# A hybrid decoder layer on one core: last tile by halves, three rows added by GpSimd, first pieces from two queues, small products on four tiles, a spill copy moved

## The chip, the cores and the metric

The kernel runs on one core of a Trainium2 chip. The metric is the device time of one execution in microseconds (us), the median of three. The engines are TensorE (PE in the profile; its weight loads are PEld), VectorE (DVE), ScalarE (ACT), GpSimd (POOL) and SyncE (SP), which here only issues DMAs. They run their own instruction streams in order and meet at semaphores.

## The reference

One layer over 512 tokens of width 1024, all in float32:

```
h = rmsnorm(x);  proj = h @ w_in                    # in slots of 256 columns
A: RWKV-7 time mixing of the first columns (8 heads of 64, delta-rule state over the tokens)
B: gated short convolution
C: attention in 3 groups of 4 heads (window 128; dilations 4 and 16), ALiBi, merged by softmax of their sums
merged = sum_i sigmoid(gate_i) * (y_i @ w_branch[rows_i])
x = x + rmsnorm(merged @ w_out)
x = x + rmsnorm((silu(gate) * up) @ w_ffn_out)      # gate, up = rmsnorm(x) @ w_ffn_in
```

The last line is the tail of the kernel: for each row of 1024 outputs z, out = x + z * rsqrt(mean(z^2) + 1e-6) * norm_ffn_post.

## The kernel before, in words

**Slots.** All weights pass through two buffers of 1 MB (w_raw, even and odd slots). For each slot SP issues the load, ScalarE rounds it to w_hi (`high`, L688), GpSimd subtracts to w_lo in four quarters (`low`, L591), and TensorE multiplies three times with 128x128 weights: high by high, high by low, low by high (`three`, L1580 to L1582). Each such product streams 512 columns. SP loads slot n when w_lo of slot n - 2 is done.

**Start.** For slots 0 and 1 the operands come in six pieces (`PIECES`). On SP's queue stand, in this order, the parameters, and then for each piece a part of x_t, of w_in slot 0 and of w_in slot 1. ScalarE casts w_hi (L723), makes b_hi from x_t (L725) and casts slot 1 (L728). VectorE makes b_lo (L1039), GpSimd w_lo (L599). TensorE first runs ten products of ones (L1636), then waits for w_lo and b_lo of a piece before its three products.

**RWKV turns.** The tokens go in four turns T of 128. TensorE's stream in a turn is written by hand: small products of the recurrence, in f32, and between them products of the projection for later slots (`fill_steps`, L1695), so that TensorE has work while other engines prepare the next small operands. Small products with 64 contraction rows are put on tiles of the array. Each f32 product leaves two records in the profile. The keys' products (L1740) and loras (L1710) use a row half with all 128 columns: two heads, or two halves, are next to each other in the stream and use different row halves. Others (L1756, L1767, L1793) use four tiles of 64x64. The attention scores (L1881) are also on row halves.

**Spills.** The filled projection tiles leave PSUM through ScalarE: `evacuate(q)` copies bank 6 or 7 to spill_buf (L774); for odd q it also issues the DMA to `spill` (L777) and runs `next_high`, the cast of a coming slot (L688). TensorE may fill tile q when q - 1 copies of the turn are made (q counted from 0). At the end of a turn ScalarE squares y (L847), waits for the variance, takes the root (L849) and then, in turns 1 to 3, runs `evacuate(9)`, (10) and (11). VectorE makes y1 from the root with a reciprocal and five operations (L1347 to L1354). TensorE, when its fill products of the turn are issued, waits for y1 and transposes it (L1829).

**Tail.** The last slot's products are ordered by token tile t, 12 each, into two PSUM banks of 512 outputs. ScalarE squares the 1024 outputs of a tile with their sum (L692) and takes the root (L694). VectorE inverts it (L1026), scales the row by root and gain (L1027) and adds x1 (L1029). ScalarE then issues the store (L1012). The four tiles go through VectorE one after the other.

Of the kernel before, what the change touches and what calls it, by code (L numbers as in the profile page):

```python
# [25 lines left out]
def hybrid_layer(nc, x, norm_mix_post, norm_ffn_pre, norm_ffn_post, w_in, rwkv_w_up, rwkv_a_up, rwkv_g_up,  # L26
                 rwkv_ln_w, rwkv_ln_b, w_branch, w_out, w_ffn_in, w_ffn_out, x_t, channel_params, out, spill):
    F = mybir.dt.float32
# [71 lines left out]
    S_X, S_SIGMA, S_Z, S_EPS, S_SCRAP = 0, 8, 16, 60, 56  # L100

    with ExitStack() as ctx:
# [13 lines left out]
        w_lo = fixed("w_lo", [P, 2, SLOT], R)  # L116
        a_hi = fixed("a_hi", [P, KT, SEQ], R)
# [209 lines left out]
        row_ready = sem("row_ready")  # L327
# [96 lines left out]
        row_ones = chunk_run[:, 0:P]  # L424
        z_of = lambda t: ps[:, 2 * t:2 * t + 2].rearrange("p a b -> p (a b)")
# [32 lines left out]
        def _(sp):  # L458
# [19 lines left out]
            sp.dma_start(params[:, 0:N_PARAMS], channel_params).then_inc(params_loaded, 16)  # L478
            xt = x_t.rearrange("(k p) t -> p k t", p=P)
            for i, (k0, k1) in enumerate(PIECES):  # L480
                sp.dma_start(x_ct[:, k0:k1], xt[:, k0:k1]).then_inc(piece_loaded[i], 16)
                sp.dma_start(half8(0)[:, k0:k1], wi[0][:, k0:k1]).then_inc(piece_loaded[i], 16)
                sp.dma_start(half8(1)[:, k0:k1], wi[1][:, k0:k1]).then_inc(second_loaded[i], 16)
# [83 lines left out]
            sp.wait_ge(out_stored, 16 * NT)  # L567
# [14 lines left out]
        def _(pool):  # L582
# [87 lines left out]
            with pool.Fori(S_REST // 2 + 1, N_SLOTS // 2, 1) as i:  # L670
                for b in range(2):
                    low(i * 2 + b, b)

# [4 lines left out]
        def _(act):  # L678
# [37 lines left out]

            act.wait_ge(eps_ready, 1)
# [31 lines left out]
            def rwkv(T):  # L749
# [97 lines left out]
                s.activation(y2[:], y1[:], ACT.Square).then_inc(y_sq.sem, 1)  # L847
                need(y_var)
# [3 lines left out]
                if T > 0:  # L852
                    evacuate(9)
# [153 lines left out]
            for t in range(NT + 1):  # L1007
                if t < NT:
                    z_root_of(t, 1, N_SLOTS)
                if t > 0:  # L1010
                    act.wait_ge(row_ready, t)
                    act.dma_start(out[0].rearrange("(t p) d -> t p d", p=P)[t - 1], x1[:, t - 1]).then_inc(out_stored, 16)  # L1012
# [5 lines left out]
        def _(dve):  # L1018
# [4 lines left out]
            def add_normed(t, xin, gain, dst, done):  # L1023
# [3 lines left out]
                link(v.scalar_tensor_tensor(out=row[:], in0=z_of(t), scalar=stat[:, S_Z + t:S_Z + t + 1], in1=gain[:],  # L1027
                                            op0=ALU.mult, op1=ALU.mult))
                v.tensor_tensor(dst[:, t], xin[:, t], row[:], ALU.add).then_inc(done, 1)  # L1029
# [538 lines left out]
            for t in range(NT):  # L1568
                add_normed(t, x1, gain_ffn, x1, row_ready)
# [544 lines left out]
```

## Time and profile before

| | us |
|---|---|
| median of 3 runs | 968.93 (967.5 to 969.11) |
| the profiled execution | 967.39 |
| its span, first to last instruction | 965.7 |
| TensorE busy | 951.7 |
| VectorE, ScalarE, GpSimd busy | 529.2, 379.8, 432.6 |

The span is what the trace covers; the execution is 1.69 us longer. In the trace a line of the timeline gives the start, the duration, the engine, the source line, what is written from what, and in brackets how long the engine was idle before it and what ended the wait. Products on TensorE overlap their successors, so a product of 512 columns shows some 0.39 us while the next starts 0.23 us behind it. How long a piece of TensorE's stream takes is therefore read from start to start.

### The profile page before, as it was taken

The numbers are of one execution on the slowest core, as the hardware profiler recorded it, in microseconds if no ns is written. First come the engines' busy times: TensorE is split into PE (matmuls) and PEld (weight loads), VectorE is DVE, ScalarE is ACT, GpSimd is POOL, SyncE is SP. The second block draws the span as 40 slices with busy tenths as digits, with TensorE's granted clock in tenths as the row PEclk, the third lists the DMA queues.
The fourth block names the chain that finished last, engine by engine and source line by source line (L and its number), as shares of the span: only waits on it lengthen the run. The fifth ranks groups of instructions, "written<-read, shape, count | busy, mean of one in ns | idle before, by whom it ended". The sixth has DMA issues, their size and how long they took to land.

```text
span 965.7 us, 15061 instructions
## 1 busy us (share of the span) xinstructions
PE 951.7 (99%) x6138; PEld 770.9 (80%) x6138; DVE 529.2 (55%) x729; ACT 379.8 (39%) x518; POOL 432.6 (45%) x349
## 2 busy tenths in 40 slices
PE   9999999999999999999999999999999999999996
PEld 7887877887787788777778888888888888888885
DVE  5877876856577755889667639633333343300004
ACT  6424516533651562346653426523322233212112
POOL 4874424433272253343044754454455445544450
PEclk9999999999999999999999999999999999999999
DMA  8333322332333273237164652234333342233212
GB/s 279 115 99 119 104 94 88 131 132 69 128 133 111 87 252 135 74 126 267 68 218 152 240 189 73 77 98 114 102 87 87 97 117 90 88 104 114 88 44 87
DMA packets 107766, 117.74 MB, mean 122 GB/s; under 512 B 2880, under 2 KB 86848, under 8 KB 107712
## 3 DMA queue, kind: packets, MB, share of 16 engines
q1 hardware_dynamic: 99792, 100.70, 32.6%
q10 hardware_dynamic: 7920, 16.25, 4.4%
q8 instruction: 41, 0.67, 0.3%
q14 instruction: 13, 0.11, 0.0%
HBM read 100.70 MB, written 16.25 MB: 121 GB/s over the span
## 4 chain that ended last, share of the span: by engine, by line
issue 37%; PE 36%; POOL 22%; DVE 2%; ACT 1%; DMA 0%; POOLq 0%; SPq 0%; DVEq 0%; ACTq 0%
POOL w_lo L591 22%; PE ps L1580 12%; PE ps L1581 12%; PE ps L1582 12%; DVE x_ct L1135 1%; DVE row L1027 1%; DVE x L1029 1%; DVE rstd_x L1058 0%; DMA w_raw<-w_in 0%; DVE proj L1065 0%; ACT w_hi L688 0%; POOL wide_mask L638 0%; ACT L694 0%; ACT squares L692 0%; POOLq L652 0%
## 5 line engine op out<-in xcount | busy, mean ns | idle before, releaser
L591 POOL TENSOR_TENSOR w_lo<-w_raw,w_hi 128x512 fp32r<-128x512 f32 x296 | 411.5, 1420 | 495.0 <-ACT w_hi L688 494.6
L688 ACT CAST w_hi<-w_raw 128x2048 fp32r<-128x2048 f32 x74 | 141.1, 1906 | 146.2 <-PE ps L1582 123.3
L1695 PE MATMUL ps<-a_hi,w_hi 128*128 128x512 f32 x384 | 156.9, 409 | 1.0 <-ACT spill_buf L774 0.9
L1580 PE MATMUL ps<-a_hi,w_hi 128*128 128x512 f32 (+1 forms) x400 | 152.9, 382 | 0.2
L1582 PE MATMUL ps<-a_hi,w_lo 128*128 128x512 f32 (+1 forms) x400 | 152.2, 381 | 0.0
L1581 PE MATMUL ps<-a_lo,w_hi 128*128 128x512 f32 (+1 forms) x400 | 152.2, 381 | 0.0
L1695 PE MATMUL ps<-a_lo,w_hi 128*128 128x512 f32 x384 | 151.7, 395 | 0.0
L1695 PE MATMUL ps<-a_hi,w_lo 128*128 128x512 f32 x384 | 151.5, 394 | 0.0
L1580 PEld LDWEIGHTS ps<-a_hi,w_hi 128*128 128x128 f32 x400 | 75.2, 188 | 15.9 <-POOL w_lo L591 1.3
L1695 PEld LDWEIGHTS ps<-a_hi,w_hi 128*128 128x128 f32 x384 | 72.1, 188 | 19.2 <-issue 2.2
L1581 PEld LDWEIGHTS ps<-a_lo,w_hi 128*128 128x128 f32 x400 | 75.2, 188 | 14.3
L1582 PEld LDWEIGHTS ps<-a_hi,w_lo 128*128 128x128 f32 x400 | 75.2, 188 | 14.2
L1695 PEld LDWEIGHTS ps<-a_lo,w_hi 128*128 128x128 f32 x384 | 72.1, 188 | 16.3 <-issue 1.7
L1695 PEld LDWEIGHTS ps<-a_hi,w_lo 128*128 128x128 f32 x384 | 72.1, 188 | 15.8 <-ACT xs L831 0.7
L1550 DVE TENSOR_TENSOR f_gate<-ps,g_up 128x512 f32<-128x512 f32 x22 | 15.2, 691 | 115.5 <-PE ps L1582 115.2
L995 ACT ACTIVATE f_sig<-f_gate 128x512 f32<-128x512 f32 x22 | 13.9, 632 | 151.7 <-DVE f_gate L1550 151.7
L1581 PE MATMUL ps<-w_lo,f_hi 128*128 128x512 f32 x176 | 68.5, 389 | 0.0
L1580 PE MATMUL ps<-w_hi,f_hi 128*128 128x512 f32 x176 | 68.5, 389 | 0.0
L1582 PE MATMUL ps<-w_hi,f_lo 128*128 128x512 f32 x176 | 68.5, 389 | 0.0
L1026 DVE RECIPROCAL stat<-stat 128x1 f32<-128x1 f32 x4 | 0.6, 158 | 109.3 <-ACT stat L694 109.3
L774 ACT COPY spill_buf<-ps 128x512 f32<-128x512 f32 x36 | 21.0, 583 | 64.5 <-PE ps L1695 64.3
L1559 DVE TENSOR_TENSOR f_lo<-f_act,f_hi 128x512 f32 x22 | 27.1, 1230 | 23.7 <-ACT f_hi L1000 23.7
(319 smaller groups left out, 1524.8 us busy)
## 6 DMA issues: line engine op xcount, KB each, us to landing
w_raw<-w_in SPq DMA_DIRECT2D x32, 1024.0 KB, 5.1
w_raw<-w_ffn_in SPq DMA_DIRECT2D x44, 512.0 KB, 4.6
spill<-spill_buf ACTq DMA_DIRECT2D x27, 512.0 KB, 3.7
w_raw<-w_ffn_out SPq DMA_DIRECT2D x11, 1024.0 KB, 4.9
w_raw<-w_branch SPq DMA_DIRECT2D x5, 1024.0 KB, 8.2
g_ab<-spill SPq DMA_DIRECT2D x8, 512.0 KB, 4.7
w_raw<-w_out SPq DMA_DIRECT2D x4, 1024.0 KB, 7.4
proj<-spill SPq DMA_DIRECT2D x1, 3072.0 KB, 14.9
```

What stands on the lines that cost most here:

```text
L591: g.tensor_tensor(w_lo[:, b, c], w_raw[:, b, c], w_hi[:, b, c].bitcast(F), ALU.subtract).then_inc(lo_ready, 1)
L688: s.copy(w_hi[:, b], w_raw[:, b]).then_inc(hi_ready, 1)
L774: s.copy(spill_buf[:, b, half], ps[:, 6 + half]).then_inc(spill_copied, 1)
L995: s.activation(f_sig[:], f_gate[:], ACT.Sigmoid).then_inc(silu_sig, 1)
L1027: link(v.scalar_tensor_tensor(out=row[:], in0=z_of(t), scalar=stat[:, S_Z + t:S_Z + t + 1], in1=gain[:], op0=ALU.mult, op1=ALU.mult))
L1029: v.tensor_tensor(dst[:, t], xin[:, t], row[:], ALU.add).then_inc(done, 1)
L1550: v.tensor_tensor(f_gate[:], ps[:, bank], row_scale[:], ALU.mult).then_inc(f_gate_ready, 1)
L1559: v.tensor_tensor(lo_[:, i, b], f_act[:], hi_[:, i, b].bitcast(F), ALU.subtract).then_inc(f_lo_ready, 1)
L1580: t_.matmul(dst, w0, a0, start=first, stop=False)
L1581: t_.matmul(dst, w0, a1, start=False, stop=False)
L1582: return t_.matmul(dst, w1, a0, start=False, stop=last)
L1695: last = t_.matmul(ps[:, 6 + half], w[:, kt, half * P:(half + 1) * P], a, start=(kt == 0 and step == 0), stop=(kt == KT - 1 and step == 2))
```

## The change

Four edits in one diff.

1. **Tail.** For tiles 0 to 2 VectorE only inverts and scales the row (into two buffers in turn); GpSimd adds x1, and SP issues the store. The last tile's products are ordered by halves of 512 outputs. ScalarE squares the halves apart; the first half's mean goes into the bias of the root. VectorE multiplies each half by the gain, and at the end by the root with x1 added, in two halves; SP stores the two halves. ScalarE takes one scratch root ahead of the tail.
2. **Start.** The first piece of w_in (slots 0 and 1) and the parameters are issued from ScalarE's queue, the x_t pieces and the rest from SP's. TensorE runs the two high by high products of piece 0 when w_hi and b_hi are there, and the other four when the low parts are.
3. **Four tiles.** The keys' products, loras and scores write 64 output rows each, in place of 128, with twice as many products; four next to each other are on four 64x64 tiles.
4. **Spill copy.** In the last turn `evacuate(9)` stands between the squares of y and the root.

```diff
+                if i > 0:
+                    sp.dma_start(half8(0)[:, k0:k1], wi[0][:, k0:k1]).then_inc(piece_loaded[i], 16)
+                    sp.dma_start(half8(1)[:, k0:k1], wi[1][:, k0:k1]).then_inc(second_loaded[i], 16)
...
+            for t in range(NT - 1):
+                pool.wait_ge(row_scaled, t + 1)
+                g.tensor_tensor(x1[:, t], x1[:, t], norm_rows[t % 2][:], ALU.add).then_inc(row_ready, 1)
...
+            act.dma_start(first_part(0), first_rows[0][:, 0:1]).then_inc(piece_loaded[0], 16)
+            act.dma_start(params[:, 0:N_PARAMS], channel_params).then_inc(params_loaded, 16)
+            act.dma_start(first_part(1), first_rows[1][:, 0:1]).then_inc(second_loaded[0], 16)
             act.wait_ge(eps_ready, 1)
...
                 s.activation(y2[:], y1[:], ACT.Square).then_inc(y_sq.sem, 1)
+                if T == NT - 1:
+                    evacuate(9)
                 need(y_var)
                 s.activation(small[:, 48:48 + NH], small[:, 48:48 + NH], ACT.Sqrt).then_inc(y_std.sem, 1)
                 if T < NT - 1:
                     lora_inputs(T + 1)
-                if T > 0:
+                if 0 < T < NT - 1:
                     evacuate(9)
...
+            s.activation(stat[:, S_SCRAP:S_SCRAP + 1], stat[:, S_EPS:S_EPS + 1], ACT.Sqrt)
+            for t in range(NT - 1):
+                z_root_of(t, 1, N_SLOTS)
+            t = NT - 1
+            act.wait_ge(z_half_done, 1)
+            s.activation(squares[:, 0:SEQ], z_of(t)[:, 0:SEQ], ACT.Square, accum_out=stat[:, S_HALF:S_HALF + 1]).then_inc(half_squared, 1)
+            act.wait_ge(slot_used, N_SLOTS)
+            s.activation(squares[:, SEQ:D], z_of(t)[:, SEQ:D], ACT.Square, accum_out=stat[:, S_Z + t:S_Z + t + 1]).then_inc(z_squared, 1)
+            act.wait_ge(z_squared, 2 * NT)
+            act.wait_ge(half_bias, 1)
+            s.activation(stat[:, S_Z + t:S_Z + t + 1], stat[:, S_Z + t:S_Z + t + 1], ACT.Sqrt, bias=stat[:, S_HALF + 1:S_HALF + 2],
+                         scale=1.0 / D).then_inc(z_root, 1)
...
+            for t in range(NT - 1):
+                if t >= 2:
+                    dve.wait_ge(row_ready, t - 1)
+                root_inverted(t)
+                v.scalar_tensor_tensor(out=norm_rows[t % 2][:], in0=z_of(t), scalar=stat[:, S_Z + t:S_Z + t + 1], in1=gain_ffn[:],
+                                       op0=ALU.mult, op1=ALU.mult).then_inc(row_scaled, 1)
+            t, halves = NT - 1, (slice(0, SEQ), slice(SEQ, D))
+            dve.wait_ge(row_ready, t - 1)
+            dve.wait_ge(half_squared, 1)
+            v.tensor_scalar(stat[:, S_HALF + 1:S_HALF + 2], stat[:, S_HALF:S_HALF + 1], 1.0 / D, NORM_EPS,
+                            ALU.mult, ALU.add).then_inc(half_bias, 1)
+            v.tensor_tensor(norm_rows[t % 2][:, halves[0]], z_of(t)[:, halves[0]], gain_ffn[:, halves[0]], ALU.mult)
+            dve.wait_ge(z_squared, 2 * NT)
+            link(v.tensor_tensor(norm_rows[t % 2][:, halves[1]], z_of(t)[:, halves[1]], gain_ffn[:, halves[1]], ALU.mult))
+            root_inverted(t)
+            for c in halves:
+                row_out(t, c)
...
+            pe.wait_ge(piece_hi_ready, 1)
+            pe.wait_ge(b_hi_ready, 1)
+            first_high()
...
-                        for half in range(2):
-                            last = t_.matmul(ps[:, half, c], lora_up[own[half], c], xm[own[half], RT - 2], start=True, stop=True)
+                        for side in range(2):
+                            for half in range(2):
+                                last = t_.matmul(ps[own[side], half, c], lora_up[own[half], c][:, own[side]], xm[own[half], RT - 2],
+                                                 start=True, stop=True)
...
-                    for c in range(2):
+                    for c, side in ((0, 0), (0, 1), (1, 0), (1, 1)):
                         for h in (2 * j, 2 * j + 1):
-                            last = t_.matmul(ps[:, mt_bank(h), col:col + P], heads(bkd, h)[:, c * P:(c + 1) * P],
+                            last = t_.matmul(ps[own[side], mt_bank(h), col:col + P], heads(bkd, h)[:, kb:kb + HD],
                                              heads(ar, h)[:, c * P:(c + 1) * P], start=True, stop=True)
...
-                        for e in range(2):
+                        for side, e in ((0, 0), (0, 1), (1, 0), (1, 1)):
-                            last = t_.matmul(dst, q[:, n * P:(n + 1) * P], k[:, k0 * P:(n + 1) * P], start=True, stop=True)
+                            dst = ps[own[side], 2 * e + c0 // SEQ, c0 % SEQ:c0 % SEQ + width]
+                            last = t_.matmul(dst, q[:, q0:q0 + HD], k[:, k0 * P:(n + 1) * P], start=True, stop=True)
```

SP now issues the stores of rows 0 to 2 as each `row_ready` comes, and then the two halves of the last row as each `last_ready` comes.

## Rows read from the trace of the kernel before

**Rows 1.** The page, busy time, share of the span and records of TensorE.

```profile
PE 951.7 (99%) x6138; PEld 770.9 (80%) x6138; DVE 529.2 (55%) x729; ACT 379.8 (39%) x518; POOL 432.6 (45%) x349
```

**Rows 2.** Chain of waits, start: start us, us, what.

```profile
1.74 2.83 DMA w_raw<-w_in
```

**Rows 3.** Timeline, start to slot 2: start us, us, engine, line, operation.

```profile
4.95 0.61 PE L1636 MATMUL ps<-all_ones 128*128 128x128 f32 x3
...
6.69 0.47 PE L1580 MATMUL ps<-b_hi,w_hi 128*128 128x512 f32 x1 [1.13 <-DVE b_lo L1039]
...
27.11 5.03 POOL L591 TENSOR_TENSOR w_lo<-w_raw,w_hi 128x512 fp32r<-128x512 f32 x4 [3.22 <-ACT w_hi L688]
...
28.99 0.79 PE L1580 MATMUL ps<-b_hi,w_hi 128*128 128x512 f32 x1
```

**Rows 4.** Timeline of TensorE: groups of small products, each with its follower.

```profile
119.91 1.16 PE L1740 MATMUL ps<-ar,bkd 64*128 64x128 f32 x16
...
121.00 0.50 PE L1695 MATMUL ps<-a_hi,w_hi 128*128 128x512 f32 x1
...
228.33 0.69 PE L1793 MATMUL ps<-state,ar 64*64 64x64 f32 x32
...
228.96 0.50 PE L1695 MATMUL ps<-a_hi,w_hi 128*128 128x512 f32 x1
...
438.22 1.79 PE L1881 MATMUL ps<-proj 64*128 64x128 f32 x16
...
439.94 0.50 PE L1855 MATMUL ps<-a_hi,w_hi 128*128 128x512 f32 x1
```

**Rows 5.** Groups by line and shape, TensorE: count, busy us, mean ns.

```profile
L1740 PE MATMUL ps<-ar,bkd 64*128 64x128 f32 x128 | 9.3, 285 | 0.0
...
L1881 PE MATMUL ps<-proj 64*128 64x256 f32 x24 | 2.9, 376 | 0.0
```

**Rows 6.** Timeline, end of the last turn: ScalarE, VectorE, GpSimd, TensorE.

```profile
420.52 1.28 ACT L849 ACT_TABLE_LOAD   x1
...
421.82 0.21 ACT L849 ACTIVATE small<-small 128x8 f32<-128x8 f32 x1
...
422.55 0.50 PE L1695 MATMUL ps<-a_hi,w_hi 128*128 128x512 f32 x1 [0.91 <-ACT spill_buf L774]
...
422.75 0.20 DVE L1347 RECIPROCAL small<-small 128x8 f32<-128x8 f32 x1
...
422.99 1.91 ACT L688 CAST w_hi<-w_raw 128x2048 fp32r<-128x2048 f32 x1 [0.49 <-ACT spill_buf L774]
...
424.44 0.69 DVE L1351 TENSOR_TENSOR y<-y,ln_wb 128x512 f32<-128x512 f32 x1
...
424.98 4.68 POOL L591 TENSOR_TENSOR w_lo<-w_raw,w_hi 128x512 fp32r<-128x512 f32 x3 [12.16 <-ACT w_hi L688]
...
425.16 1.66 DVE L1352 TENSOR_TENSOR y<-y,y 128x512 f32<-128x512 f32 x1
...
428.58 0.66 PE L1829 MATMUL ps<-ident,y 128*128 128x128 f32 x4 [0.30 <-DVE y L1354]
```

**Rows 7.** Timeline, tail.

```profile
938.77 3.78 POOL L591 TENSOR_TENSOR w_lo<-w_raw,w_hi 128x512 fp32r<-128x512 f32 x3
...
949.09 1.03 ACT L692 ACTIVATE squares<-ps 128x1024 f32<-128x1024 f32 x1 [11.64 <-PE ps L1582]
...
950.22 1.28 ACT L694 ACT_TABLE_LOAD   x1
...
956.82 0.39 PE L1582 MATMUL ps<-w_hi,f_lo 128*128 128x512 f32 x1
...
957.41 1.28 DVE L1027 SCALAR_TENSOR_TENSOR row<-ps,stat,gain_ffn 128x1024 f32<-128x1024 f32 x1
...
961.38 1.22 DVE L1029 TENSOR_TENSOR x<-x,row 128x1024 f32<-128x1024 f32 x1
```

**Rows 8.** Stretches of the tail: us, busy by engine, granted clock, DMA share, GB/s.

```profile
961.00:962.00 1.00, 0.00 (x0) 0.00 (x0) 0.96 (x2) 0.00 (x0) 0.00 (x0) 0.50 1.00 410
```

More of the change, by code:

```diff
@@ L1567, in _ @@
             dve.wait_ge(gain_ffn_loaded, 16)
-            for t in range(NT):
-                add_normed(t, x1, gain_ffn, x1, row_ready)
+            for t in range(NT - 1):
+                if t >= 2:
[14 more added lines that the diff above has]
+                row_out(t, c)
         @block.tensor
@@ L1598, in by_channel, with by_token @@
                 return last
-            def by_token(n, b, ahi, alo, first, final, t, ks=(0, 1), ready=False):
+            def by_token(n, b, ahi, alo, first, final, t, ks=(0, 1), ready=False, halves=range(2)):
                 wh = w_hi[:, b].rearrange("p (k c) -> p k c", k=2)
@@ L1605, in by_token @@
                 for k in ks:
-                    for half in range(2):
+                    for half in halves:
                         if not ready:
@@ L1623, in turn_wide, with first_high, first_rest @@
                     last.then_inc(turned, 1)
+            def first_high():
+                for m in range(2):
+                    t_.matmul(ps[:, m], w_hi[:, 0, m * P:(m + 1) * P], b_hi[:, 0], start=True, stop=False)
+            def first_rest():
+                for m in range(2):
+                    c = slice(m * P, (m + 1) * P)
+                    t_.matmul(ps[:, m], w_hi[:, 0, c], b_lo[:, 0], start=False, stop=False)
+                    t_.matmul(ps[:, m], w_lo[:, 0, c], b_hi[:, 0], start=False, stop=False)
             def first_slots(n, ks, col_tiles):
@@ L1644, in _ @@
                     pe.wait_ge(b_lo_ready, k + 1)
-                    last = first_slots(0, (k,), range(2))
+                    if k == 0:
+                        first_rest()
+                    else:
+                        last = first_slots(0, (k,), range(2))
                 if i < TOGETHER:
@@ L2081, in _ @@
                         pe.wait_ge(f_read, N_FIN)
-                    last = by_token(S_FOUT + m, (S_FOUT + m) % 2, lambda k: f_hi[:, 2 * m + k], lambda k: f_lo[:, 2 * m + k],
-                                    m == 0, m == N_FOUT - 1, t, ready=i > 0)
+                    unit = lambda halves: by_token(S_FOUT + m, (S_FOUT + m) % 2, lambda k: f_hi[:, 2 * m + k], lambda k: f_lo[:, 2 * m + k],
+                                                   m == 0, m == N_FOUT - 1, t, ready=i > 0, halves=halves)
+                    if m == N_FOUT - 1 and t == NT - 1:
+                        unit((0,)).then_inc(z_half_done, 1)
+                        last = unit((1,))
+                    else:
+                        last = unit(range(2))
                     if m == N_FOUT - 1 and t < NT - 1:
```

43 lines of the change are left out of this document (22 added, 21 removed).

## The prediction, on record before the changed kernel was run

> **What bounds the kernel now.** Read first the page's busy shares: TensorE is busy for 951.7 of 965.7 us [rows 1], so the kernel is as long as TensorE's stream plus what stands ahead of it, behind it, and in its few stalls. The 14.0 us in which it is idle are read next from the timeline. Ahead: the first real product starts at 6.69, with 1.13 us of waiting for VectorE's b_lo, and the products that only warm the array end at 5.56 [rows 3]. Behind: the last product ends at 957.21 and the span at 965.7, 8.5 us later [rows 7]. In between there are few stalls; the two that matter here lie at 422.55 (0.91 us, for the spill copy of ScalarE) and at 428.58 (0.30 us, for y1) [rows 6]. So an edit pays in full where it shortens products or either end. It costs in full where it makes TensorE wait.
>
> **First pieces.** Before, piece 0 of x_t is issued second and that of w_in third on SP: issued at 1.74, landed 2.83 later, at 4.57 [rows 2]. Now SP begins with x_t and ScalarE's queue with the w_in piece, both at about 0.8, so that the piece lands near 3.6. ScalarE has three issues first (some 0.46 each) and then its table load and scratch activation (1.28 + 0.2), which ends near 3.7: no loss. Operands are thus 0.93 earlier: b_lo lets TensorE go at 5.76, not 6.69. The two high products need only b_hi; TensorE reaches them when the warm ones are out of its way (5.4 to 5.56) and streams them in 2 x 0.213 (512 columns at 2.4 GHz), to about 5.85. What is left starts 0.84 earlier and is 0.43 shorter: 1.27. Does it keep that? At slot 2 TensorE starts at 28.99, and GpSimd's first quarter is ready at 27.11 + 5.03/4 = 28.37 [rows 3]: 0.62 of slack. That quarter follows the transfers, which move up by 0.46 (one issue less ahead of the stream) to 0.93. So between 1.08 and 1.55 us survive. I take 1.15 us gained; bounds 0.6 (the two products still run at the pace of the warm ones, which took about twice what 2.4 GHz allows, and slot 2 waits) and 1.4. The later pieces go through SP with three issues less ahead, and no queue is longer.
>
> **Four tiles.** The count of products in keys' products, loras and scores doubles, each half as wide in its weights. A group of 16 records of 128 columns on two row halves takes 1.09 us from its first start to the next 128x128 product; a scores group of 16 records, 12 of them of 256 columns, takes 1.72 [rows 4]. The 0.63 between them is six times 128 more columns in each row half: 0.105 per 128 columns, so both halves already stream beside each other. Fixed part: 1.09 - 8 x 0.105 = 0.25. A group that runs on four 64x64 tiles, 32 records of 64 columns, takes 0.63 [rows 4]: 8 per tile at 0.053 is 0.42, fixed part 0.21. So the new group is 8 x 0.105 + 0.21 = 1.05, a gain of 0.04. Groups: 128/16 = 8 of keys' products, 4 of loras (16 records in each turn), 4 of scores [rows 5]: 16 x 0.04 = 0.6. No group lies next to another of the same tile shape, before or after, so there are as many changes of shape as before. Bound above: if all of the 0.63 grew with the columns, a new group would be 1.26 and cost 0.17; in units of 128 columns the groups are 8 + 4 + 2 x 1.75 + 2 x 2 = 19.5, so 3.3 us lost. Bound below: 1 us gained. I take 0.55 gained, for the four-tile row is the nearest of kind.
>
> The trace thus shows four tiles streaming at once at 64 columns. The Trainium skill (TensorE: Matmul & The Clock Gate, Part 3, what overlaps and what doesn't) says that a weight load overlaps running matmuls only where its row group differs. By that rule the two column tiles of a row half would take turns; the four-tile row, 0.63 where turns would need at least 0.85, speaks against it. It is a rival below, priced from rows.
>
> **The spill copy moved.** In the last turn evacuate(9) now stands ahead of the square root that y1 needs. It is three things, not one: the copy (128x512 from PSUM, 0.58 as the mean of its group on the page), its DMA issue, for which ScalarE stood idle 0.49, and the next_high behind it, a cast of 1.91 [rows 6]. What they need is there by 420.5: the bank's products ended with the half slot before, some 5 us earlier, and the cast's weights had landed. The copy is done near 421.1, so TensorE's stall of 0.91 (1.05 in its pace) goes and its last fill product ends near 427.1. But the root, with its own table load of 1.28, which started at 420.52 and 421.82, now follows the cast: cast from 421.6, table load at 423.4, root at 424.7, 2.9 later. VectorE had other work until 422.75 (0.7 of slack behind the root), so its reciprocal moves from 422.75 to 425.0: 2.25 later. Behind it five such operations lead to y1. Two that lay beside GpSimd's w_lo took 1.66, one that did not 0.69 [rows 6]. GpSimd's quarter set is now 1.4 earlier against TensorE while the chain is 2.25 later; about two and a half products lie beside it instead of two, 0.3 more. TensorE's turn of y1 stood at 428.58 and waits for exactly this chain, now until about 431.1. What is late next is thus y1, and the stall that went was in front of that wait and bought nothing. Cost 2.5 us; bounds 0 (the chain has slack that I don't see) and 2.9. TensorE idles some 3.9 us there. All that follows in the attention part hangs on y_a or on TensorE and moves along.
>
> **The tail.** Before, VectorE did reciprocal, scaled row (1.28) and add (1.22) of four rows back to back and ended at 962.60; the table load of 1.28 at 950.22 was on that path [rows 7]. Now the table is loaded earlier, in ScalarE's idle time. Row 0's root comes at 950.5, rows 1 and 2 when their tiles are done; scaled rows end near 952.1, 954.8, 957.6. GpSimd adds: its w_lo quarter of 512 columns takes 3.78/3 = 1.26 [rows 7], so 1024 take some 2.5, beside VectorE's scaled rows, which read PSUM. Adds end near 954.7, 957.4, 960.2. Last tile: the first half is squared before the last product ends; the second half near 958.0 (half of 1.03, and the read of the sum); root at 958.35. VectorE: bias at 957.7, two half products (about 0.68 each) to 959.2, reciprocal to 959.4, then two half rows: one beside GpSimd's last add, some 1.1, one alone, 0.7: 961.1, 1.5 before the old end. The stores are now SP's, in order: row 2 at 960.3, halves at 960.8 and 961.2. They are 1 MB together; at 410 GB/s [rows 8] 2.6 us from 961.2, so done near 963.8, where the old last store of 0.5 MB needed 3.1 us in all from 962.6 to 965.7. With the same rest of about 0.9 behind the data: 964.7. Gain 1.0 to 1.3; I take 1.1. Bounds: 2.0 (the stores don't queue behind each other) and 0.7 lost (each add 3.7, as in the rival).
>
> **Sum.** -1.15 - 0.55 + 2.5 - 1.1 = -0.3 us. It is made against the profiled execution, 967.39 (span 965.7 and 1.69 around it), which gives 967.1. The median of the runs, 968.93, is 1.54 above that execution; the difference carried over gives 968.6. The change gains at both ends about what it loses in the middle.
>
> **Rivals.**
> *The root is not late (chance 0.17).* Were y1's chain not longer (the table load and root ahead of the cast, or slack on VectorE), the middle would cost nothing: -2.8, 966.1. For it: TensorE has hardly a wait there now. Against it: 0.30 us of wait for y1 even before the change, ScalarE in program order, and a chain on VectorE with 0.7 of slack.
> *TensorE's clock falls in the new gap (0.15; the case on the slower side).* The granted clock is at its half level (1.2 of 2.4 GHz) in the stretch 961 to 962, after a last product that ended at 957.21 [rows 7, 8], so it had fallen within 3.8 us without products. The new gap at 427 is 3.9 us by my sum. At the start the warm products, from 1.16 to 5.56, still went at half pace at the end, and the products at 6.69 did not [rows 3]: over 4.2 us of work at half pace, 2.1 to 2.8 us lost, so +2.1 in all: 971.0. It decides from a gap about as long as the one in the tail. Against it: the gap is 0.1 longer than the bound that I can read, no more.
> *GpSimd's adds bound the tail (0.07).* If an add beside VectorE takes 3.7 (as 1.66 to 0.69 for VectorE's own), three end at 963.2 and the span 3.1 later: 0.7 lost instead of 1.1 gained, 970.4. Against it: the scaled row reads PSUM.
> *Column tiles of a row half take turns (0.03).* Each group's stream doubles: 19.5 x 0.84 = 16.4 us lost, 985.
> *The likeliest (0.55)* has its own range of 967.2 to 970.2; 0.03 is left for what I don't see.
>
> **Chances.** A difference under 0.2% (1.94 us) can't be told from none here. Faster, below 967.0: the first rival and a little of the likeliest (a tail or four tiles at their good ends), 0.25. Slower, above 970.9: two thirds of the clock case, the column tiles, and some of the likeliest and of the adds, 0.19. Same: 0.56. Range for 8 in 10: 965.7 to 971.2.
>
> **What would show it.** First product at about 5.5 and the stream whole to slot 2; groups of keys' products at 1.05, not 1.09 (0.85 more means turns); at the last turn the ScalarE order copy, cast, table load, root, no wait at the last fill, and a wait for y1 of 3 to 4 us, with the clock in it; GpSimd's adds at 2.5 each, last half row near 3.9 us behind the last product, end of the span about 7.4 behind it. The prediction is wrong if the wait for y1 is under 1 us, or if the clock falls.

## The result, and the profile after: 0.2% slower, with the clock fallen in the new gap

| | before | after |
|---|---|---|
| median, 20 runs each on one chip | 967.48 (967.0 to 969.35) | 969.64 (969.23 to 971.9) |
| ratio of after to before, 95% interval | | 1.0021 [1.0015, 1.0027] |
| the profiled execution's span | 965.7 | 967.5 |
| last product starts | 956.82 | 959.93 |
| from its end to the end of the span | 8.5 | 7.2 |

The predicted 968.6 was built on a median of 968.93, which is high: 20 runs of the kernel before give 967.48. Thirteen of these 20 took 967.0 to 967.9 and seven 968.3 to 969.4, for a reason that nothing here shows, and two of the three runs behind the prediction were of the longer kind. The fair comparison is of differences: forecast -0.3 us, measured +1.8 between the two profiled executions and +2.2 between the medians. The range held the time, but by luck: moved to the base of 967.48 it would have ended 0.1 above the result. The direction did not hold.

The page's line of TensorE, which answers to [rows 1]: 288 more records, and 0.9 us more of busy time although the span is 1.8 longer.

```profile
PE 952.6 (98%) x6426; PEld 770.4 (80%) x6426; DVE 521.3 (54%) x729; ACT 380.0 (39%) x521; POOL 440.1 (45%) x352
```

The start. First the head of the chain of waits (start, us, what), in the place of [rows 2]; then the timeline, in the place of [rows 3].

```profile
1.27 3.63 DMA params<-channel_params
```

```profile
4.92 0.40 ACT L742 CAST w_hi<-w_raw 128x256 fp32r<-128x256 f32 x1 [1.19 <-DMA params<-channel_params]
...
6.10 1.12 PE L1672 MATMUL ps<-b_hi,w_hi 128*128 128x512 f32 x2 [0.30 <-ACT b_hi L744]
...
7.06 0.40 PE L1678 MATMUL ps<-b_lo,w_hi 128*128 128x512 f32 x1
...
28.89 0.79 PE L1624 MATMUL ps<-b_hi,w_hi 128*128 128x512 f32 x1
```

The chain no longer begins with a piece of weights but with the parameters. Issued second on ScalarE's queue, they landed at 4.90; x_t's piece had landed at 3.7 and the w_in piece at 4.1, both ahead of the 4.57 of before. The two high products do start 0.59 earlier than the first product did, but stand 0.56 and 0.40 us ahead of what follows them, the pace of the warm ones or worse. The low products wait for b_lo, which is ready at 6.82 (6.54 before), and so start at 7.06. Slot 2 starts at 28.89, 0.10 earlier than before. That is within what equal starts differ by from kernel to kernel (below).

The small groups, in the place of [rows 4]:

```profile
115.76 1.10 PE L1804 MATMUL ps<-ar,bkd 64*64 64x128 f32 x32
...
116.80 0.50 PE L1757 MATMUL ps<-a_hi,w_hi 128*128 128x512 f32 x1
...
441.79 1.74 PE L1945 MATMUL ps<-proj 64*64 64x128 f32 x32
...
443.47 0.50 PE L1919 MATMUL ps<-a_hi,w_hi 128*128 128x512 f32 x1
```

The keys' products' group by shape (duration min/median/max in ns, first and last start), in the place of [rows 5], has 256 records, twice as many:

```profile
L1804 PE MATMUL ps<-ar,bkd x256: 268/269/321, 115.8 to 375.0; 64*64 64x128 f32 x128
```

A group of keys' products takes 1.04 from start to follower (1.09 before), a group of scores 1.68 (1.72).

The end of the last turn, in the place of [rows 6]:

```profile
419.23 0.63 ACT L866 ACTIVATE y<-y 128x512 f32<-128x512 f32 x1 [9.60 <-DVE y L1364]
...
419.77 0.57 ACT L793 COPY spill_buf<-ps 128x512 f32<-128x512 f32 x1
...
420.83 1.91 ACT L702 CAST w_hi<-w_raw 128x2048 fp32r<-128x2048 f32 x1 [0.49 <-ACT spill_buf L793]
...
422.76 1.28 ACT L870 ACT_TABLE_LOAD   x1
422.82 5.89 POOL L602 TENSOR_TENSOR w_lo<-w_raw,w_hi 128x512 fp32r<-128x512 f32 x4 [10.64 <-ACT w_hi L702]
...
424.05 0.21 ACT L870 ACTIVATE small<-small 128x8 f32<-128x8 f32 x1
...
424.36 0.20 DVE L1376 RECIPROCAL small<-small 128x8 f32<-128x8 f32 x1 [2.29 <-ACT small L870]
...
424.60 1.31 DVE L1377 TENSOR_TENSOR y<-y,small 128x512 f32<-128x512 f32 x1
...
425.94 1.65 DVE L1379 TENSOR_TENSOR y<-y,ln_wb 128x512 f32<-128x512 f32 x1
...
430.76 1.12 PE L1893 MATMUL ps<-ident,y 128*128 128x128 f32 x4 [4.36 <-DVE y L1383]
```

ScalarE's order is copy, cast, table load, root. The wait for the spill copy is gone and one of 4.36 us for y stands behind it. The turn of y starts at 430.76; it had been 428.58. Then the same stretch of the stream is slower too. Stretches of 2 us: length, busy of PE, PEld, DVE, ACT, POOL, then granted clock, DMA share, GB/s:

```profile
430.00:432.00 2.00, 1.24 (x5) 1.24 (x6) 1.47 (x5) 0.09 (x1) 0.23 (x1) 0.56 0.18 12
432.00:434.00 2.00, 2.00 (x7) 1.54 (x7) 1.90 (x8) 2.00 (x4) 1.17 (x3) 0.58 0.82 298
434.00:436.00 2.00, 2.00 (x10) 1.65 (x9) 1.06 (x4) 2.00 (x5) 1.63 (x4) 1.00 1.02 362
```

The granted clock is at its half level (1.2 GHz) for most of 430 to 434, behind 4.36 us without products. It fell some 3.9 us behind the end of the last product (426.41), still within the wait. From the turn of y to the first scores the stream takes 441.79 - 430.76 = 11.03; before, it took 438.22 - 428.58 = 9.64. The clock costs 1.39.

The tail, in the place of [rows 7]:

```profile
957.95 2.40 POOL L686 TENSOR_TENSOR x<-x,row_next 128x1024 f32<-128x1024 f32 x1 [0.25 <-DVE row_next L1601]
...
959.93 0.39 PE L1626 MATMUL ps<-w_hi,f_lo 128*128 128x512 f32 x1
...
962.15 2.15 DVE L1057 SCALAR_TENSOR_TENSOR x<-row_next,stat,x 128x512 f32<-128x512 f32 x2
...
963.66 1.09 SPq L577 DMA_DIRECT2D out<-x  x2
```

```profile
964.00:965.00 1.00, 0.00 (x0) 0.00 (x0) 0.30 (x1) 0.00 (x0) 0.00 (x0) 0.50 1.01 406
```

GpSimd's adds take 2.4 each. The second fence is the stretch of the last stores, in the place of [rows 8]: 406 GB/s. The last half row ends 4.0 behind the last product's end, and the span 7.2 behind it, against 8.5. The clock falls in every tail too, but not at one distance from the last product. Two of the kernels below show it, the one with four tiles and tail alone and then the one with the late w_lo on one queue; their last products ended at 956.73 and 957.15:

```profile
958.00:959.00 1.00, 0.00 (x0) 0.00 (x0) 0.93 (x3) 0.00 (x0) 1.00 (x1) 0.91 0.90 365
```

```profile
962.00:963.00 1.00, 0.00 (x0) 0.00 (x0) 0.00 (x0) 0.00 (x0) 0.00 (x0) 0.65 0.96 361
```

A mean of 0.91 puts the fall at 958.8, 2.1 behind the last product; a mean of 0.65 puts it at 962.3, 5.2 behind. In the tails of the 14 traces kept, the fall came 2.1 to 5.2 us behind the last product.

**The account.** Up to the squares of y the kernel is 0.64 earlier (419.87 to 419.23): 0.1 from the start, the other 0.54 from the small groups (12 of them at some 0.05). From the squares to the turn of y it is 2.82 longer, the clock costs 1.39, and from the first scores to the last product it is 0.46 shorter. So the last product is 3.11 later. The tail gives 1.31 back: +1.80.

### The profile page after: what moved, and what is told of

Its sections match the earlier page's. It is cut to its first block, busy times and chain, and to the rows that moved or that the text cites. A ratio compares the mean times of both kernels' runs of the same rounds, so it can differ in the third digit from the quotient of the medians.

```text
span 967.5 us, 15649 instructions
## 1 busy us (share of the span) xinstructions
PE 952.6 (98%) x6426; PEld 770.4 (80%) x6426; DVE 521.3 (54%) x729; ACT 380.0 (39%) x521; POOL 440.1 (45%) x352
## 4 chain that ended last, share of the span: by engine, by line
PE 75%; issue 13%; POOL 7%; DVE 3%; ACT 1%; DMA 0%; ACTq 0%; POOLq 0%; DVEq 0%
PE ps L1757 26%; PE ps L1624 14%; PE ps L1626 14%; PE ps L1625 14%; POOL w_lo L602 7%; PE ps L1831 1%; PE ps L1804 1%; DVE proj L1198 1%; PE ps L1794 1%; PE ps L1857 0%; PE ps L1872 0%; PE ps L1773 0%; PE ps L1780 0%; PE ps L1825 0%; DMA params<-channel_params 0%
```

## The experiments

Each was timed in five rounds beside the kernel before on one chip. Times are medians; ratios are to the kernel before, with the 95% interval.

### The spill copy back in its place

```diff
-                if T == NT - 1:
-                    evacuate(9)
                 need(y_var)
...
-                if 0 < T < NT - 1:
+                if T > 0:
                     evacuate(9)
```

> The changed kernel with evacuate(9) of the last turn behind the root again. Theory: the move made y1 2.8 us late against TensorE's stream and the wait of 4.4 us let TensorE's clock fall, for 1.4 us more. So here no wait for y1 over 0.5 us, granted clock 1.00 throughout, span 963.2 to 963.6 (967.5 before the edit), time 2 us below the kernel before. Rival: start, four tiles or tail cost the time; then the span stays at 967 or more.

Measured: 965.70, ratio 0.9978 [0.9969, 0.9987], span 964.1.

```profile
428.25 0.66 PE L1891 MATMUL ps<-ident,y 128*128 128x128 f32 x4 [0.30 <-DVE y L1381]
...
437.41 1.07 PE L1927 MATMUL ps<-ident,proj 128*128 128x128 f32 x8 [0.32 <-DMA proj<-spill]
```

The clock stays at 1.00 up to the tail, and the wait for y is 0.30. The other three parts together are worth 0.22%; with the moved copy they are a loss of 0.21%. The moved copy costs 3.4 us of span, more than its own delay of 2.8. The span was forecast as 963.2 to 963.6, so 0.5 is missing. A new wait shows as well: the stream now arrives before the loads from `spill` have landed, which SP issues when y is ready.

### The moved copy alone, on the kernel before

```diff
+                if T == NT - 1:
+                    evacuate(9)
                 need(y_var)
...
-                if T > 0:
+                if 0 < T < NT - 1:
                     evacuate(9)
```

> The kernel before with only evacuate(9) of the last turn moved ahead of the root. Theory: y's turn 2.8 us later, a wait of 4.4 us, the granted clock at half for some us behind it: span 965.7 + 2.8 + 1.2 = 969.7, time 4 us above the kernel before. Rival: it costs this only together with the earlier start or the four tiles; then 2 us or less.

Measured: 972.37 (5 runs), ratio 1.0056 [1.0042, 1.0069], span 970.2. The turn of y, and one stretch of 2 us:

```profile
431.69 0.96 PE L1831 MATMUL ps<-ident,y 128*128 128x128 f32 x4 [4.34 <-DVE y L1356]
```

```profile
432.00:434.00 2.00, 2.00 (x8) 1.71 (x7) 1.75 (x8) 1.31 (x4) 0.47 (x2) 0.50 0.63 161
```

The same wait and the same half level, without any other part of the change; the forecast span was 969.7, and slot 2 began 0.62 later here than in the kernel before (29.61, held by GpSimd's w_lo). The clock fell at 431.9, 0.2 behind the start of the turn. The stretch from the turn of y to the scores takes 11.29, 1.65 more than before.

### The gap filled with products

```diff
                 need(y_ready)
...
+                    need(y_mid)
+                    for _ in range(16):
+                        t_.matmul(ps[:, 0], a_hi[:, 0, 0:P], a_hi[:, 0], start=True, stop=True)
```

The changed kernel with 16 products in the wait for y, whose results nothing uses.

> The changed kernel with 16 further products of 512 columns (3.6 us, their result is not used) in TensorE's wait for y1 in the last turn. Theory: the wait ends at the same place, near 430.8, but the clock stays at 1.00 and the 1.4 us behind it are saved: span 966.1, time 968.2. Rival: the stretch behind the wait is slow because the other engines are late, not for the clock: span 967.5 as in the changed kernel.

Measured: 968.09, ratio 1.0003 [0.9994, 1.0012], span 966.4.

```profile
430.00:432.00 2.00, 1.24 (x9) 0.88 (x7) 1.49 (x5) 0.27 (x1) 0.23 (x1) 1.00 0.00 0
432.00:434.00 2.00, 2.00 (x10) 1.68 (x9) 1.86 (x6) 2.00 (x4) 1.29 (x4) 1.00 0.80 257
```

The clock stays at full, and from the turn of y to the scores it takes 9.66 (431.04 to 440.70), as before the change. The turn itself starts 0.28 later than in the changed kernel. So the slow stretch was the clock's and not that of late engines, the rival's reason. The clock is a cost of its own, 1.1 us of span net, and it turns no measurable difference into a slower kernel.

### The copy alone ahead of the root, cast behind it

```diff
                 if T == NT - 1:
-                    evacuate(9)
+                    evacuate(9, (0,))
                 need(y_var)
...
-                if 0 < T < NT - 1:
-                    evacuate(9)
+                if T > 0:
+                    evacuate(9, (0, 1) if T < NT - 1 else (1,))
```

Part 0 is the copy; part 1 is its DMA issue and the cast.

> The changed kernel with only the copy of evacuate(9) ahead of the root; its DMA issue and the cast stand behind the root. Theory: the cast (1.91) and the issue (0.5) are what makes y1 late; the copy alone (0.57) fits in the 0.7 that the root has. So the root is 0.6 later than at first, y1 at most 0.2, TensorE's wait of 0.9 for the copy goes and turns up as a wait of 1.0 to 1.4 for y1: span within 0.3 of the one with the move undone, near 963.4. Rival: the copy itself sets y1: span 965 or more.

Measured: 967.75, ratio 1.0000 [0.9991, 1.0009], span 964.7. Its runs spread from 966.08 to 969.16, and the profiled one (966.43) is among the shortest.

```profile
421.68 0.21 ACT L875 ACTIVATE small<-small 128x8 f32<-128x8 f32 x1
...
423.77 6.33 POOL L602 TENSOR_TENSOR w_lo<-w_raw,w_hi 128x512 fp32r<-128x512 f32 x4 [11.56 <-ACT w_hi L702]
423.83 1.77 DVE L1385 TENSOR_TENSOR y<-y,ln_wb 128x512 f32<-128x512 f32 x1
425.64 1.66 DVE L1386 TENSOR_TENSOR y<-y,y 128x512 f32<-128x512 f32 x1
...
429.02 0.66 PE L1898 MATMUL ps<-ident,y 128*128 128x128 f32 x4 [2.58 <-DVE y L1388]
```

The root is in time again and y is still late. The cast now follows the root at once (421.80, against 422.99 in [rows 6]), so GpSimd starts its w_lo 1.2 earlier too, and three of VectorE's five operations on y lie beside it instead of two. The copy was cheap; what followed it in each order was not. The span was forecast near 963.4.

In the profiled run the clock stood at 1.00 behind the wait of 2.58. The mean granted clock of the other runs says that this was not the rule: it is 0.998 in three runs (966.1 to 966.4, the profiled one among them) and 0.996 in the other eight (967.7 to 969.2). The changed kernel, where the clock fell, has 0.994 to 0.996 in all of its 20 runs, and the kernel with the copy back 0.997 to 0.999. So the clock very likely fell in this gap as well, in eight runs of eleven; no trace of one of the eight was kept.

### The whole spill step ahead of the squares

```diff
-                if T == 0:
+                if T in (0, NT - 1):
...
-                if T == NT - 1:
-                    evacuate(9)
                 need(y_var)
```

Here `evacuate(9)` stands where turn 0 has its own, before the squares, while ScalarE is idle.

> The changed kernel with evacuate(9) of the last turn ahead of the squares of y, where ScalarE stood idle for 9.6 us. Theory: copy, issue and cast fit in the idle time; no wait for the copy, y1 not late, and GpSimd's w_lo is done before the products on VectorE that lead to y1, which then take 0.69 instead of 1.66: y's turn 1 to 2 us earlier than with the move undone, span 961.5 to 962.5. Rival: the cast's weights land too late and ScalarE squares late: span no better than 963.4.

Measured: 965.61, ratio 0.9980 [0.9971, 0.9989], span 963.7.

```profile
418.81 6.01 POOL L602 TENSOR_TENSOR w_lo<-w_raw,w_hi 128x512 fp32r<-128x512 f32 x4 [6.45 <-ACT w_hi L702]
...
421.29 2.38 DVE L1371 TENSOR_TENSOR y<-uv,small 64x512 f32<-64x512 f32 x2
...
428.33 0.66 PE L1891 MATMUL ps<-ident,y 128*128 128x128 f32 x4 [1.75 <-DVE y L1381]
```

GpSimd's w_lo moves with the cast and now slows other operations of VectorE in the same chain (2.38 here, 1.38 in the changed kernel). The turn of y stays where it was with the copy back (428.33 and 428.25). The forecast span of 961.5 to 962.5 missed, and not by the rival: ScalarE squared y on time.

### That w_lo held until y is ready

```diff
-            with pool.Fori(3, S_REST // 2 + 1, 1) as i:
+            with pool.Fori(3, S_REST // 2, 1) as i:
                 for b in range(2):
                     low(i * 2 + b, b)
+            low(S_REST - 1, 0)

             pool.wait_ge(y_ready.sem, NT)
+            low(S_REST, 1)
             g.iota(step_i[:], [[-1, P]], base=0, channel_multiplier=1).then_inc(dist_ready, 1)
```

> The changed kernel with two edits at the end of the last turn: ScalarE runs evacuate(9) ahead of the squares of y instead of between squares and root, and GpSimd makes w_lo of slot 31 only after y1 is ready (before, it starts as soon as the cast is done, and then lies beside VectorE's five operations on y). My theory (what delays y is the cast ahead of the root, and what lengthens it is GpSimd beside VectorE, 0.69 to 1.66 us each): with both gone the five operations take 0.69 each, y is ready near 426, TensorE has no wait above 0.3 us at the end of the turn, its clock stays at 1.00, the spill loads are issued some 2 us earlier, and the time is 3 to 4.5 below that of the kernel before: 963 to 964.4 (span 962.0 to 963.2). Rival: TensorE is held elsewhere; w_lo of slot 31 comes 4 to 5 us later and TensorE's products of that slot wait for it, so nothing is gained over the copy alone ahead of the squares: 965.6 (span 963.7).

Measured: 966.13, ratio 0.9984 [0.9975, 0.9993], span 964.4.

```profile
426.16 5.03 POOL L602 TENSOR_TENSOR w_lo<-w_raw,w_hi 128x512 fp32r<-128x512 f32 x4 [13.84 <-DVE y L1383]
...
431.47 0.24 DVE L1146 CAST step_f<-step_i 128x128 f32<-128x128 int32 x1 [5.40 <-POOL step_i L670]
...
443.34 1.74 PE L1945 MATMUL ps<-proj 64*64 64x128 f32 x32 [1.80 <-DVE p_buf L1418]
```

My account of y was right: all five operations took 0.69, y was ready at 426.1, its turn came at 426.41, and the scores 1.2 earlier than in the version above. My time was wrong, and not for the rival's reason (TensorE's wait for w_lo was 0.6). GpSimd's iota, the seed of the attention's distance tables, stood behind the held w_lo, so VectorE's tables were late, and TensorE waited 1.80 for p_buf. The gain had become a wait 17 us further on.

### The iota ahead of that w_lo

```diff
             pool.wait_ge(y_ready.sem, NT)
-            low(S_REST, 1)
             g.iota(step_i[:], [[-1, P]], base=0, channel_multiplier=1).then_inc(dist_ready, 1)
+            low(S_REST, 1)
```

> The kernel with the late w_lo of slot 31, and GpSimd's iota (0.25 us), from which VectorE builds the distance tables of the attention, stands ahead of that w_lo instead of behind it. In the kernel with the late w_lo the turn of y came at 426.4 and the first scores at 436.8, 1.2 earlier than with the copy alone moved, but VectorE got the iota at 431.1 instead of 428.4, its tables ended at 439.9 and TensorE waited 1.80 us for p_buf. My theory (that wait is the tables' chain): it goes, the tables are done before 436.5, the last scores of the group start near 462.9 instead of 464.6, and the span is 962.8 to 963.3, some 1.2 to 1.6 below that of the late w_lo; a wait of 0.3 to 0.8 us for the spill loads or w_lo may be left. Rival: the tables are slow because they lie beside GpSimd's w_lo (0.43 for 0.23), whichever comes first, and p_buf stays late by over 1 us: span 964 or more.

Measured: 965.45, ratio 0.9981 [0.9972, 0.9990], span 963.5.

```profile
426.14 5.03 POOL L602 TENSOR_TENSOR w_lo<-w_raw,w_hi 128x512 fp32r<-128x512 f32 x4
426.28 1.22 DVE L1146 CAST step_f<-step_i 128x128 f32<-128x128 int32 x1 [0.41 <-POOL step_i L669]
427.53 1.22 DVE L1147 TENSOR_SCALAR rem_i<-step_i 128x128 int32<-128x128 int32 x1
...
428.78 1.22 DVE L1148 TENSOR_SCALAR ahead_f<-step_f 128x128 f32<-128x128 f32 x1
...
436.53 1.07 PE L1929 MATMUL ps<-ident,proj 128*128 128x128 f32 x8 [0.55 <-DMA proj<-spill]
```

The wait for p_buf fell to 0.22. The span is 0.9 below the version above, where I had said 1.2 to 1.6, and at 963.5 just outside my 962.8 to 963.3; the waits for w_lo (0.8) and the spill loads (0.55) are what is left. The rival named a real effect (VectorE's small operations take 1.22 beside GpSimd) of no consequence, as there was time.

### Four tiles and tail, with start and spill copy as before

```diff
-            act.dma_start(first_part(0), first_rows[0][:, 0:1]).then_inc(piece_loaded[0], 16)
-            act.dma_start(params[:, 0:N_PARAMS], channel_params).then_inc(params_loaded, 16)
-            act.dma_start(first_part(1), first_rows[1][:, 0:1]).then_inc(second_loaded[0], 16)
...
-            first_high()
...
-                    if k == 0:
-                        first_rest()
-                    else:
-                        last = first_slots(0, (k,), range(2))
+                    last = first_slots(0, (k,), range(2))
```

with SP's queue and `evacuate(9)` as in the kernel before.

> The changed kernel with the start's and the spill's edits undone: four tiles and tail alone. Theory: four tiles gain 0.03 to 0.04 us in each of 16 groups, 0.6 in all, the tail 1.3: span 963.8 to 964.0, so 0.5 below the tail alone, and the same within 0.2 as the kernel with only the spill move undone (964.1), since the start gave nothing. Rival: the start gave its 1.1 us and something else took it: then this kernel is a microsecond slower than that one.

Measured: 965.59, ratio 0.9984 [0.9975, 0.9993], span 963.9.

```profile
4.40 0.41 ACT L737 CAST w_hi<-w_raw 128x256 fp32r<-128x256 f32 x1 [2.09 <-DMA w_raw<-w_in]
...
28.80 0.79 PE L1617 MATMUL ps<-b_hi,w_hi 128*128 128x512 f32 x1
```

On one queue the first cast starts 0.5 earlier than on two, and slot 2 no later. Forecast and span agree (963.8 to 964.0), and with the start's part the same kernel had 964.1 (medians 965.59 and 965.70). The start's part is worth nothing that these two can tell apart.

### The tail alone

The kernel before with the tail of the changed one (GpSimd's adds, last tile by halves).

> The kernel before with the tail's edit alone. Theory: from the last product's end to the end of the span 7.2 us instead of 8.5, nothing else moves: span 964.4, time 1.3 us below the kernel before. Rival: the stores at SP's end or GpSimd's adds eat half of it: 0.6 or less.

Measured: 966.07, ratio 0.9988 [0.9979, 0.9997], span 964.5: 1.2 below the kernel before, as forecast. Its last product ends at 957.32 and its span 7.2 behind that. This and the kernel above leave 0.6 of span for the four tiles; that kernel also had a wait of 0.47 for the spill loads, which this one has not. But the two starts differ as well: here slot 2 began at 29.46, held by GpSimd's w_lo, and there at 28.80. So the 0.6 is not the four tiles' alone.

### The parameters first on SP's queue, spill copy back

```diff
+            sp.dma_start(params[:, 0:N_PARAMS], channel_params).then_inc(params_loaded, 16)
...
-            act.dma_start(params[:, 0:N_PARAMS], channel_params).then_inc(params_loaded, 16)
```

> The changed kernel with the spill move undone, and with the parameters issued first on SP again (x_t's piece 0 second there, the w_in pieces still on ScalarE's queue). Theory: the start gained only 0.1 us because the parameters, issued second on ScalarE's queue beside the big pieces, landed 3.65 us after their issue instead of 1.7, at 4.91, and held up ScalarE. Here they land near 2.5, x_t's piece near 4.1, ScalarE casts at 4.1 instead of 4.9, and slot 2 starts at 28.2 to 28.5 instead of 28.9 to 29.1: span 0.5 to 0.9 below the kernel with only the spill move undone (964.1). Rival: later pieces or GpSimd's w_lo for slot 2 limit it: slot 2 stays at 28.9 or later and the span at 964.

Measured: 965.54, ratio 0.9978 [0.9969, 0.9987], span 964.6.

```profile
4.89 0.41 ACT L742 CAST w_hi<-w_raw 128x256 fp32r<-128x256 f32 x1 [1.64 <-DMA x_ct<-x_t]
...
6.06 0.70 PE L1670 MATMUL ps<-b_hi,w_hi 128*128 128x512 f32 x2 [0.86 <-ACT b_hi L744]
...
437.93 1.06 PE L1927 MATMUL ps<-ident,proj 128*128 128x128 f32 x8 [1.20 <-DMA proj<-spill]
```

The parameters now landed at 3.0 and the w_in piece at 3.2, and x_t's piece, now issued second, took the parameters' place: it landed at 4.81, and the cast starts at 4.89, against 4.92. Slot 2 started at 28.81 and y's turn 0.37 earlier than with the parameters on ScalarE's queue (427.88 to 428.25), but TensorE waited 1.20 for the spill loads in place of 0.32. This profiled run (966.37) is the longest of eleven, so its span is no measure; the medians, 965.54 and 965.70, do not show the 0.5 to 0.9 that I had forecast. The number is the rival's, the reason is not: GpSimd's first quarter for slot 2 began at 26.57 and was done a microsecond before TensorE came to it.

### One queue, high products first, on the two later versions

```diff
-                if i > 0:
-                    sp.dma_start(half8(0)[:, k0:k1], wi[0][:, k0:k1]).then_inc(piece_loaded[i], 16)
+                sp.dma_start(half8(0)[:, k0:k1], wi[0][:, k0:k1]).then_inc(piece_loaded[i], 16)
...
-            act.dma_start(first_part(0), first_rows[0][:, 0:1]).then_inc(piece_loaded[0], 16)
```

> As the kernel with the late w_lo, but the first pieces are all on SP's queue in the order of the kernel before; only the two high products first are kept of the start. My theory (the first pieces land no earlier from two queues, since the transfers behind them share the same transfer engines; 4.57 on one queue, about 4.9 on two): the real products start a little earlier than on two queues, slot 2 starts at 28.4 to 28.6 instead of 28.8, and the span is 0.2 to 0.5 below that kernel's. Rival: slot 2 is held by GpSimd's quarter and the loads behind the first pieces, so it starts at 28.8 to 29.1 on either arrangement and the spans agree within 0.2.

> As the kernel with the iota ahead of the late w_lo, but all first pieces on SP's queue in the order of the kernel before, with the two high products first. My theory (two queues land the first pieces no earlier): slot 2 starts 0.1 earlier than on two queues, as it did with the late w_lo alone (28.94 to 29.05), and the spans agree within 0.3. Rival (that queue matters and the difference was hidden by the later wait for p_buf): the span is 0.5 or more from that of the same kernel on two queues.

Measured, with the late w_lo: 965.76, ratio 0.9981 [0.9972, 0.9990], span 964.3 (964.4 on two queues), slot 2 at 28.94 (29.05). With the iota ahead of it: 965.22, ratio 0.9974 [0.9965, 0.9983], span 963.4 (963.5), slot 2 at 28.66 (28.81). The first of these had been forecast to gain 0.2 to 0.5 of span and start slot 2 at 28.4 to 28.6; that missed, on the rival's side in the numbers. Its reason does not fit: GpSimd's quarter for slot 2 was done at 27.70 (26.44 + 1.26), 1.2 ahead of TensorE. The second came out as forecast. It has the lowest median of all kernels run; its interval overlaps those of the kernels with the copy back or ahead of the squares.

## Why the prediction was wrong

The forecast for the sum was -0.3 and the trace has +1.80. Two steps failed: the start's landing time, worth 1.05 of the miss, and the clock, which the sum put at nothing, worth 1.39. Term by term:

| term | forecast | measured | from |
|---|---|---|---|
| start | -1.15 | -0.1 | slot 2, 28.99 to 28.89 |
| four tiles | -0.55 | -1.0 | 0.54 ahead of y, 0.46 behind |
| spill copy moved | +2.5 | +2.82 | squares of y to its turn |
| clock in the gap | 0, a rival at 0.15 | +1.39 | turn of y to scores |
| tail | -1.1 | -1.31 | last product to the end |

The miss of 2.10 is 1.05 + 1.39 + 0.32 - 0.45 - 0.21.

**The start failed as a term of the sum.** Its step "so that the piece lands near 3.6" took the time from issue to landing (2.83) as fixed and moved only the issue; the w_in piece took 3.3 and landed at 4.1. That alone would have left 0.5 of gain. But the sum gave the parameters no landing time, and they came last, at 4.90, 3.63 behind their issue. It isn't the order alone: with the parameters put first, x_t's piece came last, at 4.81. The first operands were complete at 4.8 to 5.1 on two queues in either order, and at 4.3 to 4.6 on one. In all these starts the first four transfers landed in the order in which they were issued, counted over both queues: the parameters behind the second x_t piece, issued 0.01 ahead of them on the other queue. That more transfers under way at once slow each other is my reading of these arrangements; it was not measured apart.

A second, smaller step of the start failed too: the two high products were to run at 0.213 each and took 0.56 and 0.40, the pace of the warm ones, which the lower bound of 0.6 had named. In three of the kernels on two queues they took 0.70 to 0.74 together, and slot 2 started at 28.81 to 29.05 all the same, because the low products wait for b_lo. Nor was slot 2 held by GpSimd, as that bound allowed: its first quarter was done at 26.57 (25.31 + 5.02 / 4), 2.3 ahead of TensorE.

Over the eight kernels on two queues slot 2 started at 28.81 to 29.13, with that quarter done at least 1.0 ahead. Over the six on one queue it started at 28.66 to 28.99 in four, and at 29.46 and 29.61 in the kernels with the tail alone and with the moved copy alone, where GpSimd's first quarter was done only at 29.40 and 29.56. So two queues did bring GpSimd's w_lo forward and took a delay of some 0.6 out that one queue has at times; they did not make slot 2 earlier than a good start on one.

**The rival of the clock happened.** I gave it 0.15 because the tail's gap of 3.8 and mine of 3.9 differed by 0.1. That step failed: it read one fall of the clock as a bound, and the falls in the tails of the later traces lie 2.1 to 5.2 us behind the last product. The measured gap was 4.36, the level fell in it, and the cost was 1.39 (1.65 with the moved copy alone), below the 2.1 to 2.8 of my price, which had taken 4.2 us of work at half pace from the start. Here the two stretches with a mean of 0.56 and 0.58 make (0.44 + 0.42) x 2 / 0.5 = 3.4 us at the half level, the first 0.5 of them before the first product, and the other 2.9 at half pace cost about half their length. Filling the gap with products whose results go nowhere removed the loss.

**The spill step was right in mechanism.** Its sum said that the reciprocal would start 2.25 later against the squares: 422.75 - 419.87 = 2.88 before, 424.36 - 419.23 = 5.13 after, 2.25. The rest was more GpSimd beside VectorE than the 0.3 allowed: 0.57. What the prediction missed is that, once the root is in time, this pairing rules the stretch. Copy alone, everything early, or all as before: each places GpSimd's w_lo beside another part of the same chain, and the turn of y came at 429.0, 428.3 and 428.3. Only holding that w_lo back, with the copy early, moved it, to 426.1 to 426.4; holding it back with the copy in its old place was not tried.

The Trainium skill (SBUF — State Buffer, the section on SBUF's two separate sides) calls the port pair that VectorE and GpSimd share an exclusive lock, held for a whole instruction; of VectorE's operations it names those with two SBUF inputs and those in a 2-port mode. The rows of the kernel with the iota ahead fit a lock: GpSimd's quarters of 1.26 (5.03 / 4) begin at 426.14, and three operations of VectorE that take 0.23 elsewhere start 1.25 apart and last 1.22 each, one to a quarter. These three have one input each, and no row tells the mode that they ran in.

**Four tiles and tail were right in kind.** 1.04 a group was forecast as 1.05; no column tiles took turns. The term came out at nearly twice its size: 12 groups ahead of y gave 0.54 and not some 0.4, the groups of scores are six and not four (192 records now, 32 in a group), and behind y a wait of 0.17 for p_buf went as well. The six groups at some 0.04 and that wait make 0.4 of the 0.46 there. From slot 2 to the turn of y the kernel before takes 399.59, the one with four tiles and tail 399.16 and the one with the copy back 399.12: 0.43 and 0.47. The tail alone gave 1.2 of span for 1.1 forecast, and GpSimd's adds took 2.4 where 2.5 was said.

**The rival in which the root is not late** fell: the reciprocal waited 2.29 for it. So did the one of GpSimd's adds.

**What ate the gains.** With the copy back, parts worth 0.1 + 1.0 + 1.3 measured together 1.6 of span. Of the missing 0.8, 0.24 lay at the start (slot 2 at 29.13, not 28.89) and 0.32 in the wait for the spill loads. Most versions in which y's turn came earlier ended in another wait: 0.3 to 1.2 for the spill loads, 0.6 to 0.8 for w_lo, 1.1 to 1.8 for p_buf. In the last version y's turn is 2.5 earlier than in the kernel before (426.10 to 428.58) and the span 2.3 shorter, of which the tail alone is 1.2.

## What to carry to other kernels

Before an instruction is moved ahead of another on the same engine, follow everything it issues or triggers: here a copy of 0.57 took a DMA issue, a cast of 1.91 and another engine's four subtractions with it. A gap of 2 us or more that opens in TensorE's stream is not priced by its length alone: the granted clock fell in or right behind both gaps of over 4 us here, and by the runs' mean clock behind most of those of 2.6. One fall read in one trace is no bound, so count the fall in the sum, not as a rival, and look at every run's clock and not only at the profiled one's. An earlier issue is no earlier operand until the last operand of the group is named, with what stands ahead of it on all queues.

## What the runs showed that I had not expected

- Beside GpSimd's subtraction of 1.26 a quarter, VectorE's conversions of 128x128 took 1.22 to 1.47 instead of 0.23, five times as long; its products of 128x512, 1.66 instead of 0.69.
- TensorE's clock fell in a wait of 4.36 and right behind one of 4.34, and the stretches there cost 1.39 and 1.65 us. Behind a wait of 2.58 it stood at 1.00 in the run with a trace and, by the mean clock, fell in eight of eleven. In 14 tails it fell 2.1 to 5.2 us behind the last product.
- A transfer of parameters took 3.6 to 3.8 from issue to landing on the second place of ScalarE's queue, 2.2 as the first of SP's beside a second queue, and 1.7 to 2.0 as the first of SP's with one queue.
